# Two patterns of one pair of key heads, tile by tile in turn

## The chip, the cores and the metric

One core of a Trainium2 chip runs the whole program. The metric is the device time of one execution in microseconds, from the first to the last instruction with what the runtime puts around them. Inputs and outputs lie in HBM. The engines are TensorE (matmuls and transposes, into the eight banks of PSUM), VectorE, ScalarE and GpSimd for elementwise work, and SyncE, whose queue issues every DMA transfer of this kernel in program order: a transfer that has to wait for a semaphore holds up all that stand behind it.

## The reference, cut to what matters

Two sequences (256 and 512 tokens, 768 in all, six tiles of 128) go through two layers. Each layer normalises the tokens, projects them to the queries, keys, values and gates of three mixers, runs the mixers, gates their outputs, and adds the output projection. The change is about mixer C, whose heads use three patterns of keys and merge them by their softmax denominators:

```
C_PATTERNS = ((128, 1), (512, 4), (2048, 16))     # window, dilation
def dilated_mixture_attention(q, k, v, rel_bias):
    for g in range(N_C_GROUPS):
        idx = qpos[:, None] + offsets[g][None, :]
        valid = (idx >= 0) & (idx < S)
        s = jnp.einsum('bqhrd,bqkhd->bhrqk', qblk[:, :, g], kg) + biases[g]
        s = jnp.where(valid[None, None, None], s, NEG_INF)
        lse = jax.nn.logsumexp(s, axis=-1)
        p = jnp.exp(s - lse[..., None])
        outs.append(jnp.einsum('bhrqk,bqkhd->bqhrd', p, vg))
        lses.append(lse)
    alpha = jax.nn.softmax(jnp.stack(lses, axis=0), axis=0).transpose(0, 1, 4, 2, 3)
    return jnp.sum(jnp.stack(outs, axis=0) * alpha[..., None], axis=0)
```

Mixer C has 8 query heads and 2 key heads for each pattern (`KV_C` = 2), so each key head serves four query heads. Mixer A has a window of 128 tokens and 12 query heads, mixer B is dense with 12 query heads.

## The kernel before

A layer has three stages: the projection, the attention, and the output projection. The attention is a list of steps, worked through by all engines in a software pipeline. `attention_units` makes twelve units, each one key head of one pattern: first the four *quads* of mixer C's dilated patterns (unit 0 and 2 are dilation 4 for key head j = 0 and 1, unit 1 and 3 are dilation 16), then three units of mixer A, two of C's pattern of dilation 1, three of B. A quad unit has six items, one for each tile t of 128 queries, with all four heads at once; the other units have 12 items of two steps. That makes 24 quad steps (steps 0 to 23) and 192 others. The diff touches `attention_items`, which lays down the order of the items; nearly all else is worked out from it.

An item of dilation 4 is *open* (tokens of one residue mod 4 are in one tile, four heads of 128 by 128 scores, 512 columns). One of dilation 16 is *packed*: only keys of the same class count, so it has 128 columns for all heads.

TensorE at turn i of the loop does the score of step i (lines 1669, or 1674 and 1675), some pieces of the gate projection (lines 1644 to 1646, three matmuls each, `PIECES_BY` says how many are done by which turn: 14 between turns 0 and 23), the transposes of step i - 3 (line 1694), and the product with the values of step i - 4 (line 1734 open, 1715 packed). VectorE adds the bias and finds the minimum (`find_minima`: line 2225 four times for an open step; lines 2179 to 2186 for a packed one), ScalarE does the exponentials (lines 1901 and 1894). The transposed probabilities are copied out of PSUM (line 1154) by ScalarE for odd steps and by VectorE for even ones (`on_act`). The output of an open item is taken out by VectorE (`take_part`, line 2293), that of a packed one by ScalarE (`take_packed`, line 1928). Banks, `prob` and `part_out` are rings, of two banks for scores, two for transposes, two for products, four slots and eight slots. VectorE's work at turn i is `take_part` of step i - 5, `find_minima` of step i, the sums of a packed step i - 3, `pt_copy` of step i - 3.

SyncE's queue in the attention goes by items. For `it` from 4 on it does, in this order: `load_item(it)` (line 1309), which first waits until item `it - 4` is scored; `store_part` (line 1378) of the quad item nine places back; and what the tables `KEYS_AT` (`load_keys`, line 1237), `VALUES_IN_AT` (`load_values`, line 1254, or `load_blocks`, line 1273, for a packed unit), `BIASES_AT` (`load_bias`, line 1297) and `GATE_LOADS_AT` (gate weights, line 1189) give for that item. Keys and values have two slots (`KV_SLOTS`), bias sets two as well, so unit u takes the slot of unit u - 2:

```
KEYS_AT = at_items((u, UNIT_LAST[u - KV_SLOTS] + 1) for u in range(KV_SLOTS, len(ATT_UNITS)))
VALUES_IN_AT = at_items((u, UNIT_LAST[u - KV_SLOTS] + PAIR_LAG + 1) for u in range(KV_SLOTS, len(ATT_UNITS)))
BIASES_AT = at_items((b, BIAS_LAST[b - 2] + 1) for b in range(2, len(BIAS_SETS)))
```

`UNIT_LAST` is the last step of a unit, `UNIT_START` the first, `BIAS_LAST` the last step that uses a bias set, `PAIR_LAG` is 5. `at_items` turns a turn into the first item `it` whose item `it - 4` has its step at that turn or later. The scores of a unit's first step wait for its keys, `find_minima` for its bias, the first product (or the splits `values_hi` and `values_lo` in mixer A) for its values; `load_keys` itself waits until unit u - 2 has had its last score. Units 0 and 1 are loaded before the loop.

Of the kernel before, what the change touches and what calls it, by code (L numbers as in the profile page):

```python
# [44 lines left out]
KV_A, KV_B, KV_C = 3, 3, 2  # L45
# [238 lines left out]
def attention_units():  # L284
    def unit(kind, mixer, q, k, v, j, g, table, reach, bias_head, chunk):
        return dict(kind=kind, q=PLACE[q + 4 * j], k=PLACE[k + j], v=PLACE[v + j], j=j, g=g, table=table, reach=reach,
                    bias_head=bias_head, chunk=chunk + 2 * j)

    quads = [unit("Q", "C", U_QC + g * H_C, U_KC + g * KV_C, U_VC + g * KV_C, j, g, 2 * g, 0, H_A + g * H_C + 4 * j, 0)
             for j in range(KV_C) for g in (1, 2)]  # L290
    a = [unit("A", "A", U_QA, U_KA, U_VA, j, 0, 0, 1, 4 * j, 0) for j in range(KV_A)]
    c = [unit("C", "C", U_QC, U_KC, U_VC, j, 0, 1, 1, H_A + 4 * j, (H_A + H_B) // 2) for j in range(KV_C)]
    b = [unit("B", "B", U_QB, U_KB, U_VB, j, 0, None, 3, 0, H_A // 2) for j in range(KV_B)]
    return quads + a + c + b


ATT_UNITS = attention_units()
# [11 lines left out]
def packed(unit):  # L309

    return unit["kind"] == "Q" and unit["g"] == 2


def unit_items(u):
    return [(u, hp, t) for hp in ((None,) if ATT_UNITS[u]["kind"] == "Q" else (0, 1)) for t in range(TT)]


def attention_items():

    order = [x for u in range(len(ATT_UNITS)) for x in unit_items(u)]
    items, steps = [], []
    for u, hp, t in order:
        unit = ATT_UNITS[u]
        lo, hi = next(x for x in SEQ_TILES if x[0] <= t < x[1])
        a, b = max(lo, t - unit["reach"]), min(hi, t + unit["reach"] + 1)
        for r in (None,) if hp is None else (0, 1):
            first = min(max(t * P - C_REACH, lo * P), hi * P - C_KEYS) if unit["kind"] == "C" else a * P
            tiles = (1 if packed(unit) else 4) if r is None else C_KEYS // P if unit["kind"] == "C" else b - a  # L330
            steps.append(dict(item=len(items), u=u, unit=unit, kind=unit["kind"], hp=hp, t=t, r=r, a=a, first=first,
                              tiles=tiles, last=r != 0))
        items.append(dict(u=u, unit=unit, kind=unit["kind"], hp=hp, t=t, step=len(steps) - 1))
    return items, steps


ITEMS, STEPS = attention_items()

SHIFTED = sorted({x["first"] + j * P for x in STEPS if x["kind"] == "C" and x["first"] % P for j in range(x["tiles"])})
# [2326 lines left out]
```

How the kernel before makes its waits and increments, by code:

```python
        def prob_copied(eng, l, i):  # L914
            if features_first(STEPS[i]) or not on_act(i):
                eng.wait_ge(pt_dve, l * DVE_COPIES[-1] + DVE_COPIES[i])
            else:
                eng.wait_ge(pt_act, l * ACT_COPIES[-1] + ACT_COPIES[i])
# [1 line left out]
        def turn_evacuated(eng, i):  # L921
            l, s, t, b, _ = TURNS[i]
            if s == "norm":
                eng.wait_ge(norm_lo, NORM_AT[l, s, t, b] + 1)
            else:
                eng.wait_ge(turned_lo, HEAD_AT[l, s, t] + 1)
# [17 lines left out]
        def quad_taken(eng, l, quad):  # L945
            item = QUADS[quad]
            if packed(item["unit"]):
                eng.wait_ge(packed_taken, l * N_PACKED + item["packed_no"] + 1)
            else:
                eng.wait_ge(part_taken, l * (N_QUADS - N_PACKED) + item["open_no"] + 1)
# [5 lines left out]
        def bias_in(eng, l, b):  # L957
            sets = [x for x in BIAS_SETS if BIAS_NO[x] % 2 == b % 2]
            each_layer = sum(4 if x[1] is None else 2 for x in sets)
            in_layer = sum(4 if x[1] is None else 2 for x in sets if BIAS_NO[x] <= b)
            eng.wait_ge(bias_loaded[b % 2], 16 * (l * each_layer + in_layer))
# [5 lines left out]
        def stat_free(eng, pair):  # L968
# [3 lines left out]
            l, at = divmod(pair - STAT_SLOTS, N_PAIRS)  # L972
            old = PAIRS[at]
            if old["kind"] == "C":
                eng.wait_ge(merge_chain, 5 * (l * MERGES + old["merge_no"] // TT) + 5)
            else:
                eng.wait_ge(normed, l * NORMED[-1] + NORMED[old["step"]])
```

## Time and profile before

| | |
|---|---|
| median of three runs | 2769.77 us (2768.97 to 2772.97) |
| the profiled execution | 2773.48 us, span 2771.7 us |
| mean granted TensorE clock | 0.996 |
| quad steps, first quad score to first score of mixer A | 651.0 to 709.1 us, and 2028.4 to 2083.2 us |
| busy: TensorE, VectorE, ScalarE, GpSimd | 98%, 58%, 43%, 34% of the span |

A granted clock of 1.00 is the full 2.4 GHz, 0.50 is 1.2 GHz; a value between is a mean over a stretch. Engines' busy times overlap. "Releaser" is what ended an engine's idle time. A transfer's time to landing counts from the start of its issue to the semaphore that says it is there.

### The profile page before, as it was taken

What the parts mean: (1) busy time and instruction counts of PE and PEld (TensorE: products, weight loads), DVE (VectorE), ACT (ScalarE), POOL (GpSimd) and SP (SyncE); (2) the same over time, 40 slices, a digit from 0 to 9 for tenths busy, and PEclk for the clock granted to TensorE, in tenths of its full rate; (3) what the DMA queues carried; (4) which work ended last, traced back from release to release, by engine and by line L of the source; (5) the groups of instructions that cost most, each with busy time, mean ns of one, the idle gap of its engine ahead of it and who ended that gap; (6) DMA issues with size and microseconds to landing.
All of it is one profiled execution on the core that took longest, in us unless ns stands there. A gap on an engine that the chain in (4) does not pass through costs nothing. (4 is left out here: it accounts for less than half of the span.)

```text
span 2771.7 us, 43372 instructions
## 1 busy us (share of the span) xinstructions
PE 2728.9 (98%) x14505; PEld 2444.1 (88%) x14505; DVE 1614.7 (58%) x3901; ACT 1190.9 (43%) x2897; POOL 943.0 (34%) x864
## 2 busy tenths in 40 slices
PE   8999999999999999999999999999999999999999
PEld 7888899988999999988888888999889999998887
DVE  3345644434676677667743466444356766766776
ACT  4322222224565566544542222222256655664443
POOL 0333333320465377600003334333205743774000
PEclk9999999999999999999999999999999999999999
DMA  5366556658544443464524565666685345325535
GB/s 175 105 185 199 181 184 189 180 171 229 149 134 125 118 116 87 145 245 124 202 92 119 187 194 179 193 175 178 184 232 147 115 118 155 94 70 210 198 122 182
DMA packets 439415, 442.53 MB, mean 160 GB/s; under 512 B 103863, under 2 KB 333399, under 8 KB 439196
## 3 DMA queue, kind: packets, MB, share of 16 engines
q1 hardware_dynamic: 439196, 439.77, 53.0%
q8 instruction: 118, 1.93, 0.3%
q14 instruction: 101, 0.83, 0.1%
HBM read 313.91 MB, written 125.75 MB: 159 GB/s over the span
## 5 line engine op out<-in xcount | busy, mean ns | idle before, releaser
L1818 ACT CAST w_hi<-w_raw 128x512 fp32r<-128x512 f32 x640 | 397.2, 622 | 695.2 <-PE bank L1590 430.3
L1588 PE MATMUL bank<-w_hi,act_hi 128*128 128x512 f32 x1728 | 689.1, 399 | 0.0
L2099 DVE TENSOR_TENSOR w_lo<-w_raw,w_hi 128x512 fp32r<-128x512 f32 x640 | 457.8, 716 | 391.9 <-ACT w_hi L1818 389.0
L1590 PE MATMUL bank<-w_hi,act_lo 128*128 128x512 f32 x1728 | 679.0, 393 | 0.0
L1589 PE MATMUL bank<-w_lo,act_hi 128*128 128x512 f32 x1728 | 677.6, 392 | 0.0
L2548 POOL TENSOR_SCALAR prob<-prob,denom 128x256 f32<-128x256 f32 (+2 forms) x288 | 348.8, 1216 | 243.1 <-DVE denom L2263 239.8
L1590 PEld LDWEIGHTS bank<-w_hi,act_lo 128*128 128x128 f32 x1728 | 372.6, 216 | 54.0
L1588 PEld LDWEIGHTS bank<-w_hi,act_hi 128*128 128x128 f32 x1728 | 373.3, 216 | 50.0
L1589 PEld LDWEIGHTS bank<-w_lo,act_hi 128*128 128x128 f32 x1728 | 373.3, 216 | 48.8
L1644 PE MATMUL bank<-act_hi,w_hi 128*128 128x384 f32 x1024 | 348.8, 341 | 0.0
L1646 PE MATMUL bank<-act_hi,w_lo 128*128 128x384 f32 x1024 | 345.9, 338 | 0.0
L1645 PE MATMUL bank<-act_lo,w_hi 128*128 128x384 f32 x1024 | 345.6, 338 | 0.0
L1621 PE MATMUL bank<-w_hi,a_part 128*128 128x512 f32 x672 | 263.2, 392 | 5.7 <-DVE a_part L2391 3.0
L2254 DVE TENSOR_TENSOR pt_lo<-bank,pt_hi 128x256 fp32r<-128x256 f32 (+2 forms) x288 | 154.2, 535 | 188.3 <-ACT pt_hi L1920 186.2
L1622 PE MATMUL bank<-w_lo,a_part 128*128 128x512 f32 x672 | 261.7, 389 | 0.0
L1623 PE MATMUL bank<-w_hi,a_part 128*128 128x512 f32 x672 | 261.6, 389 | 0.0
L2539 POOL TENSOR_TENSOR y<-y,gains 128x256 f32<-128x256 f32 (+1 forms) x144 | 159.8, 1122 | 265.7 <-DVE y L2132 265.7
L2165 DVE TENSOR_TENSOR turned<-bank,turned 128x512 fp32r<-128x512 f32 (+2 forms) x120 | 64.8, 557 | 278.3 <-ACT turned L1885 278.2
L1885 ACT CAST turned<-bank 128x512 fp32r<-128x512 f32 (+2 forms) x120 | 55.3, 482 | 365.0 <-PE bank L1566 355.9
L1694 PE MATMUL bank<-ident,prob 128*128 128x128 f32 x1128 | 195.7, 274 | 5.7 <-POOL prob L2548 5.7
L1645 PEld LDWEIGHTS bank<-act_lo,w_hi 128*128 128x128 f32 x1024 | 193.9, 189 | 4.2
L1914 ACT ACTIVATE prob<-prob,minus_max 128x257 f32<-128x257 f32 (+2 forms) x240 | 128.2, 534 | 161.2 <-DVE minus_max L2245 160.4
(135 smaller groups left out, 4500.7 us busy)
## 6 DMA issues: line engine op xcount, KB each, us to landing
w_raw<-w_in SPq DMA_DIRECT2D x144, 512.0 KB, 4.8
w_sums<-sum_out SPq DMA_DIRECT2D x32, 1280.0 KB, 6.8
w_raw<-w_sums SPq DMA_DIRECT2D x80, 512.0 KB, 4.1
sum_in<-w_out SPq DMA_DIRECT2D x64, 512.0 KB, 5.6
heads_t<-turned SPq DMA_DIRECT2D x240, 128.0 KB, 2.4
q_t<-heads_t SPq DMA_DIRECT2D x192, 128.0 KB, 2.1
k_t<-keys_t SPq DMA_DIRECT2D x48, 384.0 KB, 5.8
w_raw<-w_out SPq DMA_DIRECT2D x32, 512.0 KB, 3.7
```

The lines of the kernel that those rows point to most:

```text
L1588: pe.matmul(acc[t][:], hi, w_hi[:, W_AT[n]:W_AT[n] + SLAB], start=(k == 0), stop=False)
L1589: pe.matmul(acc[t][:], hi, w_lo[:, W_AT[n]:W_AT[n] + SLAB], start=False, stop=False)
L1590: last = pe.matmul(acc[t][:], lo, w_hi[:, W_AT[n]:W_AT[n] + SLAB], start=False, stop=(k == KC - 1))
L1621: pe.matmul(bank[at][:], hi[:, tokens], w_hi[:, W_AT[n]:W_AT[n] + SLAB], start=(j == 0), stop=False)
L1622: pe.matmul(bank[at][:], hi[:, tokens], w_lo[:, W_AT[n]:W_AT[n] + SLAB], start=False, stop=False)
L1623: last = pe.matmul(bank[at][:], lo[:, tokens], w_hi[:, W_AT[n]:W_AT[n] + SLAB], start=False, stop=(j == KH - 1))
L1644: pe.matmul(out, hi, act_hi[:, k, tokens], start=(k == 0), stop=False)
L1645: pe.matmul(out, hi, act_lo[:, k, tokens], start=False, stop=False)
L1646: last = pe.matmul(out, lo, act_hi[:, k, tokens], start=False, stop=(k == KC - 1))
L1818: nc.scalar.copy(w_hi[:, W_AT[n]:W_AT[n] + SLAB], w_raw[:, load % W_RAW, j, :]).then_inc(w_hi_done, 1)
L2099: nc.vector.tensor_tensor(w_lo[:, W_AT[n]:W_AT[n] + SLAB], w_raw[:, load % W_RAW, j, :], w_hi[:, W_AT[n]:W_AT[n] + SLAB].bitcast(F32), ALU ...
L2548: nc.gpsimd.tensor_scalar(v, v, denom[:, pair % STAT_SLOTS, st["r"]:st["r"] + 1], None, ALU.mult)\
```

## The change

The items of unit 0 and unit 1 alternate tile by tile (open t = 0, packed t = 0, open t = 1, and so on), then those of unit 2 and 3; the rest of the list stays. Even quad steps are then open and odd ones packed. The items are the same and so is their work. All tables are worked out anew from the list: the first four values of `UNIT_START` and `UNIT_LAST` were 0, 6, 12, 18 and 5, 11, 17, 23, and are 0, 1, 12, 13 and 10, 11, 22, 23.

```diff
--- before.py
+++ after.py
@@ -319,7 +319,8 @@
 
 
 
-    order = [x for u in range(len(ATT_UNITS)) for x in unit_items(u)]
+    order = [x for j in range(KV_C) for both in zip(unit_items(2 * j), unit_items(2 * j + 1)) for x in both]
+    order += [x for u in range(2 * KV_C, len(ATT_UNITS)) for x in unit_items(u)]
     items, steps = [], []
     for u, hp, t in order:
         unit = ATT_UNITS[u]
```

## Rows read from the trace of the kernel before

**Rows 1.** The page: busy time of TensorE, share of the span, instructions.

```profile
PE 2728.9 (98%) x14505; PEld 2444.1 (88%) x14505; DVE 1614.7 (58%) x3901; ACT 1190.9 (43%) x2897; POOL 943.0 (34%) x864
```

**Rows 2.** Windows: us, then busy us (count) of each engine, granted clock, DMA share, GB/s.

```profile
651.00:709.10 58.10, 51.97 (x358) 48.30 (x356) 37.55 (x176) 30.03 (x128) 2.01 (x2) 0.89 0.83 233
709.10:715.00 5.90, 5.90 (x26) 5.50 (x25) 2.77 (x13) 2.23 (x7) 0.12 (x1) 0.65 0.31 82
2028.40:2083.20 54.80, 47.90 (x356) 44.63 (x355) 37.02 (x174) 29.38 (x127) 2.00 (x2) 0.96 0.86 246
2083.20:2088.00 4.80, 4.80 (x24) 4.62 (x23) 2.74 (x11) 2.51 (x9) 0.00 (x0) 0.78 0.36 94
```

**Rows 3.** Timeline of TensorE, layer 0: start us, duration us, line, operation.

```profile
663.82 0.61 PE L1669 MATMUL bank<-k_t,quad_t 128*128 128x64 f32 x4
664.27 0.42 PE L1644 MATMUL bank<-act_hi,w_hi 128*128 128x384 f32 x1
...
664.88 0.60 PE L1694 MATMUL bank<-ident,prob 128*128 128x128 f32 x4
665.32 1.00 PE L1734 MATMUL bank<-v_t,prob_t 128*128 128x64 f32 x8
666.13 0.39 PE L1669 MATMUL bank<-k_t,quad_t 128*128 128x64 f32 x2
```

**Rows 4.** Timeline of TensorE, layer 1: from one open score to the next.

```profile
2054.19 0.41 PE L1674 MATMUL bank<-k_t,quad_t 128*128 128x128 f32 x1
...
2055.60 0.41 PE L1674 MATMUL bank<-k_t,quad_t 128*128 128x128 f32 x1
```

**Rows 5.** Timeline of TensorE, layer 0: the first score of step 4.

```profile
658.68 0.33 PE L1674 MATMUL bank<-k_t,quad_t 128*128 128x128 f32 x1 [0.37 <-DMA quad_t<-heads_t]
```

**Rows 6.** Windows behind four waits, columns as in rows 2.

```profile
675.00:690.00 15.00, 14.27 (x72) 12.89 (x71) 8.76 (x55) 9.16 (x41) 0.00 (x0) 0.66 0.84 221
705.00:715.00 10.00, 8.61 (x34) 8.03 (x35) 4.66 (x19) 2.80 (x9) 0.12 (x1) 0.66 0.51 160
2062.00:2072.00 10.00, 8.77 (x61) 8.64 (x62) 7.06 (x35) 6.37 (x28) 0.00 (x0) 0.83 0.76 230
2077.00:2087.00 10.00, 7.41 (x38) 6.61 (x38) 4.87 (x18) 3.04 (x12) 0.00 (x0) 0.83 0.74 213
```

**Rows 7.** Timeline of SyncE's queue, layer 0: start us, us for the issues.

```profile
662.16 0.32 SPq L1309 DMA_DIRECT2D quad_t<-heads_t  x1
...
664.19 1.09 SPq L1237 DMA_DIRECT2D k_t<-keys_t  x2
...
692.66 3.71 SPq L1273 DMA_DIRECT2D blocks<-v_rows  x8
```

**Rows 8.** DMA issues, 655 to 716 us: count, KB each, median us to landing.

```profile
k_t<-keys_t SPq DMA_DIRECT2D x8, 384.0 KB, 5.8
...
v_t<-v_rows SPq DMA_DIRECT2D x2, 192.0 KB, 3.3
blocks<-v_rows SPq DMA_DIRECT2D x8, 24.0 KB, 2.5
bias<-bias_rows SPq DMA_DIRECT2D x4, 8.0 KB, 4.7
```

**Rows 9.** Landing of the `k_t` transfers, 655 to 716 us.

```profile
DMA to landing us min/median/max: 4.4/5.8/7.0
```

**Rows 10.** Timeline of VectorE, layer 0.

```profile
652.10 0.29 DVE L2225 CUSTOM_DVE_ANT_0 prob<-bank,bias 128x128 f32<-128x128 f32 x1 [3.68 <-PE bank L1675]
...
652.99 0.29 DVE L2225 CUSTOM_DVE_ANT_0 prob<-bank,bias 128x128 f32<-128x128 f32 x1
...
665.65 0.68 DVE L1154 COPY prob_t<-bank 128x512 f32<-128x512 f32 x1
666.36 0.42 DVE L2293 COPY part_out<-bank 128x256 f32<-128x256 f32 x1
666.78 0.29 DVE L2179 TENSOR_TENSOR prob<-bank,bias 128x128 f32<-128x128 f32 x1
```

## The prediction

> **What bounds the kernel now.** I read the page first: TensorE is busy for 98% of the span [rows 1]. Nothing else is near that, so a wait counts only where it stops TensorE, and then it counts in full. The edit touches the list of the first 24 items of each layer's attention, so I looked next at the two stretches in which TensorE works on them, from the first quad score to the first score of mixer A. They last 58.1 us in layer 0 and 54.8 us in layer 1 [rows 2]. The reader should see two things there: TensorE is idle for 6.1 and 6.9 us, which is rare in this kernel, and the granted clock is 0.89 and 0.96, and still 0.65 and 0.78 in the few microseconds behind. This is the only part with something to gain. TensorE's own work per step comes next: a packed score, a gate piece, the four transposes and the four products of an open item follow each other in 2.31 us (0.45, 0.61, 0.44, 0.81) [rows 3], and an open score with a packed item's transpose and product take 1.41 us [rows 4]. Last I read SyncE's queue and its transfers, since a step's queries, keys, bias and values all come through that one queue, in the order of the item list: `load_keys` for the second pair of key heads is issued in 1.09 us [rows 7] and lands 5.8 us after issue (4.4 to 7.0) [rows 8, 9].
>
> **What the change removes.** At best all that those stretches lose now. Layer 0: 58.10 - 51.97 = 6.1 us idle, 58.1 x 0.11 = 6.4 us through the clock, and 5.9 x 0.35 = 2.1 us just behind: 14.6 us. Layer 1: 6.9 + 54.8 x 0.04 + 4.8 x 0.22 = 10.2 us [rows 2]. Together 24.8 us. A regular mix of long and short steps may well cure it: the present waits are for a queue that falls behind short steps and for an engine that falls behind long ones. I credit the whole, and put what may remain under a term of its own.
>
> **What it adds: late loads.** No instruction is added. But `UNIT_LAST` of the first four units changes from 5, 11, 17, 23 to 10, 11, 22, 23, while `UNIT_START` changes from 0, 6, 12, 18 to 0, 1, 12, 13. Only two units' keys fit at a time, and the queue asks for the next only when the unit before last has had its last step. Worked through `at_items`: keys and bias of unit 2 stood at item 10 of the queue and now stand at item 15; unit 3 stays at 16; unit 4 goes from 22 to 27. Values: unit 2 from 15 to 20, unit 3 stays at 21, unit 4 from 27 to 30. Item n's own load waits for the score of item n - 4, so keys of unit 2 are now requested after score 11 and needed by score 12; keys of unit 3 after score 12, needed by score 13 (it was 18); keys of unit 4 after score 23, needed by 24; values of unit 2 after score 16, needed by product 12, which is TensorE's next task but a transpose; values of unit 3 after score 17, needed by product 13. Six loads that had about five steps of cover have less than one. Each price below is for one layer: issue, landing, less the work TensorE still has.
>
> Ahead of them in the queue are one query load (0.32 us) and one part store (taken alike, some 0.4 us with its pause): 0.9 us from the score to the first key transfer, 0.55 us to the second [rows 7], 5.8 us to land, 0.1 us to start.
> Keys of unit 2: 0.9 + 0.55 + 5.8 + 0.1 = 7.3 us, less a gate piece, four transposes and a packed product (0.61 + 0.44 + about 0.25, and a little pipelining): **5.9** (4.5 to 7.1).
> Keys of unit 3: the same 7.3 us, less one transpose and an open product (0.9 us): **6.4** (5.0 to 7.6).
> Bias of unit 3 goes out behind those keys and lands 4.7 us later [rows 8]; VectorE waits at `find_minima` 13, and behind that wait stand `pt_copy` 10 and with it TensorE's product 10: **1.1** (0 to 2).
> Values of unit 2: 0.9 + 3.3 [rows 8] + 0.1 less 0.2: **4.1** (3.4 with the 2.5 us of the small blocks, 5.3 with the keys' shortest landing).
> Blocks of unit 3: 0.9, then eight issues in 3.71 us, the last 3.2 us after the first [rows 7], 2.5 us to land [rows 8], 0.1, less a gate piece and four transposes (0.9): **5.9** (5.4 to 6.7).
> Keys of unit 4: as unit 2: **5.9** (4.5 to 7.1).
> Values of unit 4: after score 29 0.9 + 3.3 + 0.1, then the splits on ScalarE and VectorE, about 1.1 us for both (the wider copy takes 0.68 [rows 10]), against 3.3 us of gate pieces, transposes and score 30: **2.1** (1.2 to 3.2).
> First queries: item 4's load lets TensorE start at 658.68 [rows 5] whatever stands before it, and the shorter steps 1 and 3 leave it less to do until then: **1.6** (0 to 2.5).
> The sum is 33.0 us a layer (24.0 to 41.5).
>
> **The clock.** After today's waits the granted clock sits between its two levels of 2.4 and 1.2 GHz on average: 0.66 over 15 us, 0.66 over 10, 0.83 over 10 and 0.83 over 10 [rows 6], which costs 5.1, 3.4, 1.7 and 1.7 us, on average 3.0. The new waits are longer than those. Three of them (unit 3's keys, unit 3's blocks, unit 4's keys) are followed by plain work and I charge 3.0 each; the other two long ones run into the next wait, which hides half of it: 1 each. That is 11 us a layer (5.1 to 17.3).
>
> **VectorE.** Open items now have even numbers, so all their 512-wide copies fall to VectorE (0.68 us [rows 10]), none to ScalarE. A pair of steps costs it 0.89 + 4 x 0.29 with pauses (1.25) + 0.68 + 0.42 [rows 10] and 0.28 for the packed sums: 3.5 us, against 1.41 + 2.31 = 3.7 us of TensorE. That just fits, at no cost, while the two stay in step; for a missed beat, a weight split (three in this stretch) or a part store that is late for its slot I charge 3 us a layer (0 to 8).
>
> **Sum.** 33.0 + 11 + 3 = 47.0 us a layer, 94.0 in all, less 24.8: +69 us. The profiled execution took 2773.5 us around a span of 2771.7, 3.7 above the median of 2769.8; the difference is set on the median: **2839 us**. All low ends give 2 x 29.1 - 24.8 = +33, or 2803; all high ends 2 x 66.8 - 24.8 = +109, or 2879.
>
> A page speaks on this too. The Trainium skill, "DMA: Bandwidth & Descriptors", Anatomy of one DMA, has about 2.0 us fixed plus the bytes at 436 GB/s (for the GpSimd path). By it both key transfers together would be down in an estimated 3.8 us where rows 8 and 9 show 5.8 after a second issue 0.55 us late, and the values in 2.4 instead of 3.3: 9 us a layer less, and a result of about 2820. The rows were taken beside this kernel's other traffic, so I stay with them.
>
> **Rivals.** (1) *Only the score waits show.* The value loads arrive in time because the queue has caught up by then and TensorE is held elsewhere. Per layer 1.6 + 5.9 + 6.4 + 1.1 + 5.9 = 20.9, clock 7, beats 3: 30.9; twice, less 24.8: +37, 2807 us. For it: their landings are short. Against it: the request hangs on scores 16 and 17, not on the queue's leisure. (2) *VectorE sets the pace.* If a pair takes 4.5 us instead of 3.7, 12 pairs cost 9.4 us a layer, of which 3 are charged: +13 in all, 2852 us. For it: 3.5 against 3.7 leaves nothing. (3) *Faster.* The even mix gives back 24.8 us, and the loads hide as they do now: 2 x (1.6 + 3) - 24.8 = -16, 2754 us. It would need keys that land within the 1.3 us that TensorE still has, or a request that goes out earlier than I read. It decides from the point where waits and clock cost under 12.4 us a layer; the two key waits at steps 12 and 13 alone come to 9.5 at their shortest. (4) *They cancel* near that point, within 5.5 us.
>
> **Chances.** Forecast 0.74, rival 1 0.13, rival 2 0.08, rival 3 0.03, rival 4 0.02. A measurement here tells about 0.2% (5.5 us) from no change. Faster 0.03, same 0.02, slower 0.95. The range runs from the low ends and rival 1 to some way above rival 2: 2803 to 2865.
>
> **What would show it.** In the chain of waits: TensorE idle until a transfer of `k_t` some 5 to 7 us before score 12, again before 13, again before 24 (the first of mixer A), in both layers; idle for `v_t` before product 12, for `blocks` before product 13. The stretches should be about 85 us long, with the granted clock low behind each wait, and between the waits a pair of steps should take about 3.7 us with TensorE back to back; the waits for `quad_t` in the middle of packed runs should be gone. From mixer C on nothing should differ. I am wrong if keys of unit 2 are in SyncE's timeline before score 11 is done; if the waits are there but short, the landing is mis-sized; if steps 4 to 11 already run late, VectorE is.

## The result

The changed kernel takes 2844.74 us (median of 4 runs, 2839.69 to 2847.02) where the kernel before takes 2771.37 beside it (2768.97 to 2780.37): ratio 1.0254, interval 1.0235 to 1.0273, some +70 us. The forecast was +69 and 2839, with 0.95 on slower. The profiled execution took 2839.69 us around a span of 2837.9, 66.2 us more than the span before. It is the fastest of the four; where the other three lose 5 to 7 us more, at a mean granted clock of 0.980 or 0.981 against 0.982, no trace shows.

The page of the changed kernel comes first. TensorE's busy time rose by only 16.3 us against [rows 1], with the same number of instructions. Most of the loss is therefore idle time, and the rest is the same work at a lower clock.

```profile
PE 2745.2 (97%) x14505; PEld 2458.7 (87%) x14505; DVE 1616.5 (57%) x3901; ACT 1189.5 (42%) x2897; POOL 943.3 (33%) x864
```

The windows from the first quad score to the first score of mixer A, and the 20 us behind, in both layers (columns as in [rows 2]; the stretches end at the same score as there, but two of the four products that still lie behind that score are now open ones):

```profile
650.60:735.10 84.50, 56.50 (x342) 52.33 (x340) 39.39 (x179) 30.58 (x132) 2.02 (x2) 0.72 0.60 162
735.10:755.00 19.90, 17.00 (x99) 16.33 (x100) 7.81 (x34) 6.70 (x22) 6.64 (x7) 0.89 0.61 161
2058.90:2144.10 85.20, 55.72 (x342) 51.65 (x340) 39.24 (x179) 30.59 (x132) 2.02 (x2) 0.75 0.59 160
2144.10:2164.00 19.90, 17.20 (x98) 16.55 (x99) 7.74 (x33) 6.70 (x22) 6.64 (x7) 0.88 0.62 162
```

The stretches grew by 26.4 and 30.4 us. That is 56.8 of the 66.2; the other 9.4 lie close behind, in mixer A. In layer 0 a load of gate weights issued at 765.54 before stands at 796.13 now, 30.6 us later, and the keys issued at 1034.09 stand at 1064.70, still 30.6 us later: between the two nothing more is lost. In the two stretches TensorE is idle for 28.0 and 29.5 us, where it was idle for 6.1 and 6.9, and the granted clock is 0.72 and 0.75 instead of 0.89 and 0.96.

These are the waits of TensorE in the changed kernel: what it waited for, the total in us, how often, the longest.

```profile
PE bank L1675 <- issue: 13.6, 2, 6.9
PE bank L1670 <- issue: 12.3, 2, 6.2
PE bank L1681 <- issue: 10.9, 2, 5.5
PE bank L1735 <- DMA v_t<-v_rows: 10.3, 2, 5.9
PE bank L1716 <- DMA blocks<-v_rows: 8.5, 2, 4.3
...
PE bank L1750 <- issue: 6.0, 4, 2.9
```

None of the first five is in the kernel before; each comes twice, once in each layer. (Lines are one higher than before.) L1675 is the open score, here that of step 12; L1670 the packed score, here step 13; L1681 the first score of mixer A, step 24; L1735 and L1716 are the products of steps 12 and 13. Where the row says only "issue", the profile names no releaser. SyncE's timeline does: keys are requested at 671.50, just as TensorE runs out of work, and again at 681.84, after score 12.

```profile
670.66 0.32 SPq L1310 DMA_DIRECT2D quad_t<-heads_t  x1
671.03 0.43 SPq L1379 DMA_DIRECT2D part_rows<-part_out  x1
671.50 1.09 SPq L1238 DMA_DIRECT2D k_t<-keys_t  x2
...
681.84 1.10 SPq L1238 DMA_DIRECT2D k_t<-keys_t  x2
```

TensorE's side of it (timeline, start and duration in us, the idle time before in brackets):

```profile
671.52 0.60 PE L1716 MATMUL bank<-blocks,prob_t 128*128 128x256 f32 x2
679.01 0.45 PE L1675 MATMUL bank<-k_t,quad_t 128*128 128x128 f32 x1 [6.89 <-issue]
...
688.86 1.03 PE L1670 MATMUL bank<-k_t,quad_t 128*128 128x64 f32 x4 [6.08 <-issue]
...
705.97 0.87 PE L1735 MATMUL bank<-v_t,prob_t 128*128 128x64 f32 x3 [4.36 <-DMA v_t<-v_rows]
...
714.94 1.19 PE L1716 MATMUL bank<-blocks,prob_t 128*128 128x256 f32 x2 [4.26 <-DMA blocks<-v_rows]
...
735.01 0.55 PE L1681 MATMUL bank<-k_t,q_t 128*128 128x256 f32 x1 [5.40 <-issue]
```

From the first key issue at 671.50 to the score at 679.01 are 7.5 us: a second issue 0.55 us later, and a landing near the top of its spread (4.2 to 6.9 us for `k_t` in this stretch). What the transfers took, 655 to 735 us (KB each, median us from issue to landing), answers to [rows 8]:

```profile
k_t<-keys_t SPq DMA_DIRECT2D x6, 384.0 KB, 5.6
...
v_t<-v_rows SPq DMA_DIRECT2D x1, 192.0 KB, 3.5
blocks<-v_rows SPq DMA_DIRECT2D x8, 24.0 KB, 1.9
```

The granted clock in four windows of layer 0: before the first new wait, from the end of that wait on, behind that, and at the start of mixer A.

```profile
660.00:671.40 11.40, 11.25 (x90) 11.01 (x91) 9.23 (x45) 7.22 (x32) 0.00 (x0) 1.00 0.70 203
679.00:719.00 40.00, 25.30 (x104) 23.58 (x105) 12.03 (x55) 8.31 (x34) 0.00 (x0) 0.50 0.42 107
719.00:730.00 11.00, 10.43 (x81) 9.63 (x80) 9.10 (x37) 7.75 (x34) 0.00 (x0) 1.00 0.54 167
735.00:739.40 4.40, 4.39 (x18) 4.30 (x19) 0.91 (x5) 1.27 (x4) 0.00 (x0) 0.51 0.02 5
```

Before the wait the alternating steps run at 2.4 GHz; behind it TensorE works at 1.2 GHz for 40 us, through the next three waits and all the work between. Then it is back at 2.4 GHz until the wait for unit 4's keys, and low once more for 4.4 us behind that. At half rate 25.3 us of work should have taken 12.65, and 4.39 should have taken 2.2: 14.8 us for layer 0. In layer 1 three stretches at 0.50, 0.52 and 0.54 (2087.5 to 2101, 2112 to 2133, 2144 to 2149.5) hold 7.25, 16.75 and 5.50 us of work, by the same reckoning 14.2 us.

Now the books close: the waits of both layers come to 61.1 us (worked out below), the clock to 29.0, and the 24.8 us that the kernel before lost here are gone or included: 65.3, against 66.2 between the spans.

### The profile page after: what moved, and what is told of

The parts are those of the page before. It is cut to its first block and busy times, and to the rows that moved or that the text cites. A ratio compares the mean times of both kernels' runs of the same rounds, so it can differ in the third digit from the quotient of the medians.

```text
span 2837.9 us, 43376 instructions
## 1 busy us (share of the span) xinstructions
PE 2745.2 (97%) x14505; PEld 2458.7 (87%) x14505; DVE 1616.5 (57%) x3901; ACT 1189.5 (42%) x2897; POOL 943.3 (33%) x864
## 5 line engine op out<-in xcount | busy, mean ns | idle before, releaser
L1645 PEld LDWEIGHTS bank<-act_hi,w_hi 128*128 128x128 f32 x1024 | 194.3, 190 | 4.1
```

Source lines behind the costliest of these rows:

```text
L1645: pe.matmul(out, hi, act_hi[:, k, tokens], start=(k == 0), stop=False)
```

## The experiments

Ratios are to the kernel before on the same chip, each kernel timed in five rounds. What an expectation calls the changed kernel is the one above.

### One pair at a time

**e1_first_pair** alternates units 0 and 1 only.

```diff
-    order = [... for j in range(KV_C) for both in zip(...) ...]
+    order = [x for both in zip(unit_items(0), unit_items(1)) for x in both]
+    order += [x for u in (2, 3) for x in unit_items(u)]
...
```

> Only units 0 and 1 alternate; units 2 and 3 stay one after the other. Late-load theory: unit 2's keys (asked for after score 11, needed by score 12) and unit 2's values are late as in the changed kernel, unit 3's and unit 4's loads are early again. TensorE idle some 6.8 us before score 12 and 4 to 6 us before product 12 in each layer, none before score 13, product 13 or score 24: +28 us against the kernel before (18 to 38). Pace theory (alternation itself is slow, for VectorE or for the copies that all fall to one engine): half of the whole loss, about +36 us, spread over steps 0 to 11 and none of it at step 12.

Measured: 2797.73 us, ratio 1.0092 (1.0066 to 1.0117), about +25. Its waits:

```profile
PE bank L1676 <- issue: 14.3, 2, 7.7
PE bank L1736 <- DMA v_t<-v_rows: 11.4, 2, 5.7
```

**e2_second_pair** is the mirror: units 0 and 1 in sequence, 2 and 3 alternating.

> Only units 2 and 3 alternate. Late-load theory: unit 2's loads are early, unit 3's keys (before score 13) and blocks (before product 13) and unit 4's keys (before score 24) and values are late: some 18.7 us idle and 9 us of low clock a layer, less the 8 us that this half lost before: +39 us (28 to 50), and with the first pair's alone it adds up to the whole loss of 73 us within 10. Pace theory: +36 us, the same as the first pair's alone.

Measured: 2819.12 us, 1.0165 (1.0139 to 1.0191), about +46. Its waits:

```profile
PE bank L1671 <- issue: 14.4, 2, 7.6
PE bank L1717 <- DMA blocks<-v_rows: 12.1, 2, 6.4
...
PE bank L1682 <- issue: 8.5, 2, 4.4
```

Each half brings exactly the waits of the loads whose slots its pair holds on to: the first pair unit 2's keys and values; the second unit 3's keys and blocks and unit 4's keys and values (the last as two waits of up to 2.6 us at L1751). 0.92% and 1.65% make 2.57%, the whole change 2.54%: the halves add up.

### How much head start a load needs

**e3_one_ahead**, **e4_three_ahead** and **e8_four_ahead** let the open unit run one, three or four tiles ahead of the packed one. Its slot then comes free that many steps earlier.

```diff
-    order = [... for j in range(KV_C) for both in zip(...) ...]
+    order, ahead = [], 3          # 1 in the first, 4 in the last
+    for j in range(KV_C):
+        wide, narrow = unit_items(2 * j), unit_items(2 * j + 1)
+        order += wide[:ahead] + [x for both in zip(wide[ahead:], narrow) for x in both] + narrow[TT - ahead:]
...
```

> Alternating, but the open item runs one tile ahead of the packed one, so each late load is asked for one score earlier (two scores before its use instead of one). Late-load theory: each wait is shorter by one step, 1.5 to 2.3 us, so 17 us idle a layer instead of 30, and less low clock: +32 us (15 to 50). Pace theory: five sixths of the alternation is left, so about +60 us.

Measured: 2813.74 us, 1.0138 (1.0114 to 1.0162), about +38. The waits for keys of units 2 and 3 fell to 4.51 and 5.18, 4.42 and 3.94 us, that for values to 2.82 and 3.13, the blocks' to 0.6, and that for unit 4's keys to 1.69 and 3.67.

> The open item runs three tiles ahead, so each load is asked for four scores before its use, some 8 us, against 7.3 us from request to landing. Late-load theory: no wait on k_t, v_t or blocks above 1 us; the time falls to that of the kernel before or under it, -10 us (-25 to +6). Pace theory: half of the alternation is left, about +36 us.

Measured: 2772.83 us, 0.9986 (0.9972 to 1.0000). That is 4 us of gain where I had expected 10. Three waits for keys are above the 1 us that I had allowed: one of 1.20 us before the first score of unit 2 in layer 1 (the profile names no releaser, but SyncE had issued these keys 8 us before), and two for unit 4's keys, shown below. Small ones for queries (1.37 and 0.40 us) and blocks (0.56 us) remain beside them.

```profile
PE bank L1684 <- DMA k_t<-keys_t: 2.3, 1, 2.3
PE bank L1684 <- issue: 2.3, 1, 2.3
```

> Four tiles ahead: five scores between request and use, one third of the alternation left. Late-load theory: no wait on keys or values above 0.5 us; -6 us against the kernel before (-20 to +5). If the alternation itself helps by its even mix, this has less of it than three tiles ahead, and comes out no faster than that.

Measured: 2775.27 us, 1.0007 (0.9995 to 1.0019). One tile ahead gives back 32 us, three the whole loss, and a fourth nothing more: all new key waits are gone, but small waits for queries, for VectorE's copies and a low clock (0.78 over layer 1's stretch of 63.1 us) take their place. I had asked for more than the order can give.

### The same order without the late loads

**e5_alt_loads_out** lets units 2 and 3 compute on the keys, bias and values of units 0 and 1, so those loads are left out; all steps and their work stay. **e6_seq_loads_out** does the same in the order before. Both leave the right keys, bias and values of units 2 and 3 out, so only their times are of use.

```diff
-                        load_keys(l, u)
+                        if u > 3:
+                            load_keys(l, u)
...
-                        load_values(l, u)
+                        if u > 3:
+                            load_values(l, u)
...
-                        load_bias(l, b)
+                        if b > 3:
+                            load_bias(l, b)
```

> The changed kernel, but units 2 and 3 use the keys, bias and values of units 0 and 1: their loads are left out, and with them the four waits inside the quad steps; unit 4's keys and values stay late. Late-load theory: of 30 us idle a layer about 8 are left (before score 24 and in mixer A), with some 3 us of low clock and 3 to 5 of small waits, against 12.4 that the kernel before loses: +8 us in all (-10 to +20). Pace theory: the loss is in the steps themselves, so +50 us or more stays.

Measured: 2772.05 us, 0.9993 (0.9983 to 1.0003). Its windows:

```profile
650.20:701.90 51.70, 44.36 (x342) 41.57 (x341) 38.61 (x179) 30.27 (x132) 2.00 (x2) 1.00 0.74 215
2025.60:2077.30 51.70, 44.45 (x342) 41.65 (x341) 38.76 (x179) 30.19 (x132) 2.02 (x2) 0.96 0.74 216
```

and the only key wait left, before score 24, for the load that stayed:

```profile
PE bank L1684 <- issue: 11.4, 2, 5.8
```

> The kernel before with the same loads left out (units 2 and 3 use the keys, bias and values of units 0 and 1). It tells what leaving them out is worth by itself. Late-load theory: in the old order they were hidden, only the traffic beside the query loads gets less: -6 us (-15 to +3). If the transfers themselves fill the DMA engines and set the pace, more than -20 us.

Measured: 2763.47 us, 0.9963 (0.9948 to 0.9978).

The same 24 alternating steps take 51.7 us instead of 84.5, at a clock of 1.00 in layer 0; 5.7 us of that are the wait for unit 4's keys, so the steps themselves need 46.0. The order costs nothing as an order, and the 73 us of the whole hang on the loads of units 2 and 3. Two things keep this pair from being the whole proof. Leaving these loads out also takes their traffic away, which e6 prices at 10 us in the order before. And with them out the alternating order is 8.6 us slower than the old one (2772.05 against 2763.47): its waits for unit 4's keys, 11.4 us, and values, up to 3.3 us each, are still there. That it is the lateness and not the traffic is shown by e4 above and e9 below, in which every load is made and the loss is gone too.

### Keys ahead of the queries in the queue

**e7_three_ahead_keys_first** is e4 with an item's `load_keys` put before its query load and part store.

> Three tiles ahead, and in SyncE's queue the keys of the next unit are asked for before the item's own queries and the part store, 0.8 us sooner. Late-load theory: the wait of 2.3 us before score 24 shrinks to about 1.5 in each layer, some low clock behind it goes: 2 to 5 us under three tiles ahead alone. Pace theory: no difference.

Measured: 2771.80 us, 0.9992 (0.9981 to 1.0003), so no gain over e4: a miss. The key wait before score 24 did go, but one of 1.41 us for that item's own queries (`q_t`) stands there instead, layer 1's stretch was granted 0.86, and products wait for VectorE's copies (4.3 us over the kernel at L1738, 3.0 in e4).

### The slots filled by halves

**e9_alt_half_loads** keeps the alternating order and loads keys and values of units 2 to 4 in two halves of three tiles, each asked for as soon as its own three tiles have been used. The two small packed bias tables get a tile of their own, so that bias no longer needs a slot of the pair. **e10_seq_half_loads** is its control: the same loads in the order before.

```diff
+def freed(u, g, lag):
+    if u > 4:
+        return UNIT_LAST[u - KV_SLOTS] + lag
+    return min(i for i, st in enumerate(STEPS) if st["u"] == u - KV_SLOTS and st["t"] == 3 * g + 2) + min(lag, V_LAG + 1)
...
-KEYS_AT = at_items((u, UNIT_LAST[u - KV_SLOTS] + 1) for u in range(KV_SLOTS, len(ATT_UNITS)))
+KEYS_AT = at_items(((u, g), freed(u, g, 1)) for u in range(KV_SLOTS, len(ATT_UNITS)) for g in range(2))
...
-BIASES_AT = at_items((b, BIAS_LAST[b - 2] + 1) for b in range(2, len(BIAS_SETS)))
+BIAS_SLOT = [0, None, 1, None] + [b % 2 for b in range(4, len(BIAS_SETS))]
```

> Alternating as in the changed kernel, same work and same two slots, but keys and values are loaded in two halves of three tiles, each as soon as the steps of those tiles are done, and the packed units' small bias tables lie apart, so that unit 2's bias can be loaded at the start. Each half is asked for five scores or more before its use. Late-load theory: no wait of TensorE on k_t, v_t or blocks above 0.5 us, quad stretches of some 47 us at full clock instead of 84: 2751 us, -20 against the kernel before (-28 to -8). Pace theory: +50 us or more stays. DMA theory (the transfers fill the engines): stretches stay at 55 us, time as before.

Measured: 2766.38 us, 0.9979 (0.9965 to 0.9993). All waits for `k_t`, `v_t` and `blocks` are gone with the alternating order intact, which is what the theory needed; but the gain was 6 us where I had forecast 20. What took the rest is in its waits and in SyncE's timeline:

```profile
PE bank L1700 <- DMA quad_t<-heads_t: 5.8, 3, 2.8
```

```profile
674.15 1.18 SPq L1253 DMA_DIRECT2D k_t<-keys_t  x2
675.37 2.13 SPq L1313 DMA_DIRECT2D bias<-bias_rows  x2
677.55 0.43 SPq L1327 DMA_DIRECT2D quad_t<-heads_t  x1
```

The queries of step 14 stand behind 3.3 us of issues of one item. TensorE waits 2.73 and 2.80 us for them, and is granted 0.71 over the 17 us from 683 on. In layer 1 of this profiled execution TensorE also waits 1.70 us for VectorE, until 2026.89, and is granted 0.55 over the next 5 us and 0.64 over 8 more. VectorE had itself been idle for 5.28 us until a transfer landed. It is no wait for queries, and e11's profiled execution does not have it.

> The same half loads and bias places in the order of the kernel before. Late-load theory: its loads were hidden already, so this is the control: 0 us (-8 to +5). If the half loads and not the order made the alternating one fast, both gain alike.

Measured: 2778.41 us, 1.0001 (0.9980 to 1.0023), with a wide spread from 2762 to 2788. In its profiled execution, the slowest of the twelve, layer 1 paid dearly for one wait of 2.25 us for `quad_t` at 2037.56. The 20 us behind it, with TensorE never idle:

```profile
2040.00:2060.00 20.00, 20.00 (x86) 19.25 (x84) 9.72 (x31) 3.87 (x11) 0.00 (x0) 0.50 0.62 174
```

Five gate pieces lie in these 20 us; this is the first matmul of the first:

```profile
2042.81 0.67 PE L1667 MATMUL bank<-act_hi,w_hi 128*128 128x384 f32 x1
```

**e11_alt_half_loads_spread** is e9 with the wide bias of number 4 asked for at another item of the queue, so that it no longer piles up in front of step 14's queries.

```diff
-BIASES_AT = at_items((b, BIAS_LAST[BIAS_OLD[b]] + 1) for b in range(4, len(BIAS_SETS)))
+BIASES_AT = at_items((b, 18 if b == 4 else BIAS_LAST[BIAS_OLD[b]] + 1) for b in range(4, len(BIAS_SETS)))
```

> The alternating kernel with half loads, with one load moved: the bias of mixer A's first half, which held SyncE's queue for 2.1 us right behind unit 2's second half of keys, goes out seven items later. In the kernel with half loads TensorE's one long wait in each layer, 2.7 to 2.8 us for item 14's queries, stands there, with low clock for 10 us behind it. Queue theory: that wait falls under 1 us and the low clock goes, 8 us less in each layer, 2752 us, -20 against the kernel before (-26 to -8). If instead the DMA engines are simply full at that place, the wait stays and the time is that of the kernel with half loads, -6.

Measured: 2760.49 us (2758.90 to 2762.00), 0.9953 (0.9940 to 0.9966): 13 us faster than the kernel before, some 84 than the changed one; I had forecast 20. Its windows and what is left of the query waits (1.5 us at the longest, where I had expected under 1):

```profile
650.20:701.80 51.60, 49.02 (x342) 46.15 (x340) 38.36 (x179) 30.08 (x131) 2.02 (x2) 0.90 0.83 243
2021.70:2071.00 49.30, 45.73 (x340) 42.88 (x339) 37.77 (x178) 29.80 (x130) 2.01 (x2) 0.97 0.86 255
```

```profile
PE bank L1700 <- DMA quad_t<-heads_t: 1.8, 2, 1.5
```

Once its loads have cover, the alternating order thus gains about half of the 24.8 us of losses. Half loads alone, in the order before, were worth nothing (e10); whether they would be with the bias moved as well was not tried, so how much of e11's 13 us is the order's alone stays open.

### Other work put into the waits

**e12_gate_work_in_the_waits** leaves the order and loads of the changed kernel alone, and moves the 14 gate pieces, which are spread over the quad steps, to steps 11 and 12, where TensorE waits.

```diff
-    cost = [3 if packed(st["unit"]) else {"Q": 1}.get(st["kind"], 8) for st in STEPS]
+    cost = [(24 if i in (11, 12) else 0) if st["kind"] == "Q" else 8 for i, st in enumerate(STEPS)]
```

> The changed kernel with its late loads, but the 14 gate pieces of the quad steps all stand behind scores 11 and 12, seven each, where TensorE waits for the keys of units 2 and 3. Late-load theory: 12 of the 14 pieces, 6.2 us, now run inside the two waits instead of beside other steps, the waits shrink from 6.8 and 6.1 to some 3.3 and 2.6 us, and the clock does not fall before the values' wait, 2 to 5 us more: -8 to -11 us a layer, 2825 us against 2844 (2818 to 2833). If the time from request to landing were not what TensorE waits for, moving its work would change nothing, or lengthen the other steps' latencies and cost time.

Measured: 2852.41 us, 1.0284 (1.0267 to 1.0300), 8 us above the changed kernel where I had forecast some 20 below: a miss. The waits before scores 12 and 13 did shrink, from 25.9 us in all to 10.3:

```profile
PE bank L1675 <- issue: 6.6, 2, 4.5
```

But the steps that had lost their gate pieces ran at half the clock. Windows of layer 0: until the clock had fallen, while it was low, its last half microsecond, and behind its rise, which comes before the first gate piece:

```profile
651.10:657.00 5.90, 5.01 (x35) 4.49 (x35) 4.66 (x26) 3.26 (x16) 0.00 (x0) 0.85 0.62 178
657.00:674.50 17.50, 17.50 (x80) 16.96 (x80) 10.28 (x46) 8.64 (x37) 2.00 (x2) 0.50 0.62 183
675.00:675.50 0.50, 0.50 (x5) 0.50 (x5) 0.00 (x0) 0.00 (x0) 0.00 (x0) 0.50 0.02 4
676.00:676.90 0.90, 0.90 (x11) 0.90 (x10) 0.90 (x10) 0.40 (x2) 0.00 (x0) 1.00 0.25 23
```

```profile
676.97 0.42 PE L1645 MATMUL bank<-act_hi,w_hi 128*128 128x384 f32 x1
```

TensorE had no idle time in those 17.5 us; the longest wait in the 6 us before was one of 0.70 us for VectorE, which ended at 653.22. In the changed kernel the same steps, with their gate pieces, kept 1.00. Layer 1 is alike: 0.50 from 2070 to 2090, and the first gate pieces, from 2091.90 on, run at 1.2 GHz too. Over the two stretches TensorE is busy for 67.4 and 66.8 us with the work that took 56.5 and 55.7 in the changed kernel: 22 us more, against 12 us less in the waits for late loads (61.6 us in all there, 49.6 here).

## Why the prediction was right

Forecast +69 us, measured about +70 by the ratio and +73 by the medians. The mechanism was the forecast one: without the loads of units 2 and 3 the alternating order costs nothing (e5), and neither with them when they are asked for earlier (e4, e9).

**Late loads.** Six waits stand where the six were forecast. Forecast, then layer 0 and layer 1, in us: keys of unit 2 5.9, measured 6.89 and 6.67; keys of unit 3 6.4, measured 6.08 and 6.20; values of unit 2 4.1, measured 4.36 and 5.92; blocks of unit 3 5.9, measured 4.26 and 4.25; keys of unit 4 5.9, measured 5.40 and 5.46; values of unit 4 2.1, measured 2.90 and about 2.7. Together 30.3 forecast, 29.9 and 31.2 measured. The values of unit 2 in layer 1 lie above their range of 3.4 to 5.3: they landed in 5.0 us, where I had taken 3.3. The queue had issued a 512 KB load of gate weights (L1190) just ahead of them, 2 us before; in layer 0, where `v_t` landed in 3.5 us, that load was 4.5 us ahead. That it slowed them is likely, but was not tried.

```profile
2104.80 0.43 SPq L1190 DMA_DIRECT2D w_raw<-w_in  x1
...
2106.87 0.38 SPq L1255 DMA_DIRECT2D v_t<-v_rows  x1
```

The blocks lie below their range of 5.4 to 6.7, for two reasons that the rows show: they land in 1.9 us instead of 2.5, and TensorE had 2.0 us of work left (708.7 to 710.68) instead of 0.9, since by then it worked at the low clock. The half clock hides a part of the very transfers that brought it about.

**The two small terms.** First queries 1.6 and bias of unit 3 1.1: measured 0.3 and nothing. Both were too high, by 2.4 us a layer. Product 10 stands in the timeline without a wait, right behind the transpose.

**The clock.** Forecast 11 us a layer (5.1 to 17.3), measured 14.8 and 14.2. The term was inside its range but under-sized, and the step that failed is the reasoning behind it: I priced one recovery per wait from [rows 6], at a mean of 3.0 us. In layer 0 the clock did not recover between the first four waits: one low stretch of 40 us ran through the work between them, and only before unit 4's keys was it up again. In layer 1 it recovered once more, between the waits for unit 3's keys and unit 2's values (0.97 from 2101 to 2106).

**VectorE.** Forecast 3 us a layer for missed beats, measured none to speak of. In the 11.4 us before the first new wait TensorE is busy for 11.25 (the window above). One pair of steps there, from an open score to the next:

```profile
663.78 0.41 PE L1675 MATMUL bank<-k_t,quad_t 128*128 128x128 f32 x1
...
664.80 0.39 PE L1645 MATMUL bank<-act_hi,w_hi 128*128 128x384 f32 x1
...
666.75 0.42 PE L1645 MATMUL bank<-act_hi,w_hi 128*128 128x384 f32 x1
...
668.05 0.41 PE L1675 MATMUL bank<-k_t,quad_t 128*128 128x128 f32 x1
```

That pair takes 4.27 us because it holds two gate pieces; the one before it, with one, takes 3.63, against 3.7 forecast. VectorE's 3.5 us fit beneath. Rival 2 is out, and e5 says the same for the whole section.

**What it removes.** All 24.8 us were credited. The waits for `quad_t` in front of packed scores, 7.7 us in all in the chain of waits of before, are down to 0.2, as forecast. This is their row in the kernel before:

```profile
PE bank L1669 <- DMA quad_t<-heads_t: 7.7, 4, 3.3
```

Of the idle time the credit was near the truth: outside the forecast waits TensorE is idle for 1.0 us in each stretch, where it was idle for 6.1 and 6.9. The other 11.8 us of the 24.8 were low clock, and the trace cannot tell old low clock from new. e11 gets 13 us in all, after its own remaining waits and a clock of 0.90 and 0.97.

**The sum.** The errors cancelled: the clock 3.5 us a layer too low, first queries, bias and beats together some 5 too high. That the total came within 2 us of the ratio's +70 is in that part luck; that the six waits came out right is not. Rival 1, only the score waits, fell with the rows of `v_t` and `blocks`: 10.3 and 8.5 us. Rival 3 needed a request that goes out earlier; e4, e9 and e11 are that rival made true, and e11 reached -13 of its -16 us. e4 and e8, at 0.9986 and 1.0007, are where rival 4 stood: losses and gains cancel.

**The page's figure.** The Trainium skill, "DMA: Bandwidth & Descriptors", Anatomy of one DMA, gave an estimated 3.8 us for the two key transfers of a unit (its fit is for the GpSimd path) and with it some 2820 us in all. The rows after show a median of 5.6 us for `k_t` and 3.5 for `v_t` from SyncE's queue beside this kernel's traffic. The measured landings decide, and the sum by them was nearer by some 20 us.

## What to carry to other kernels

Two units that alternate hold both of two slots until the pair's end, so that nothing can be prefetched for the next pair: when two streams are interleaved, count for each load the steps between the release of its slot and its first use, before counting what the mix gains. The cure is to release and fill slots by parts (here halves, with the bias loads moved, which turned +73 us into -13) or to let one stream lead; and then see what else the queue issues at the same place, since 3.3 us of issues in front of one query load cost e9 about half its gain. Filler work moved into a wait is missed where it came from: in e12 the steps without it ran at half the clock, and the kernel lost more than the shorter waits gave.

## What the runs showed of the hardware

- After one wait, work in which TensorE was never idle stayed at the lower level of 1.2 GHz for long: 17.5 us of quad steps without gate pieces in e12, 20 us in e10. It can be short as well: behind the 5.40 us wait before mixer A's first score the changed kernel was back at 2.4 GHz from 739.4 on, 4.4 us after that score began. That the gate pieces are what keeps it up is only a reading of e12 against the changed kernel, and two rows speak against the simple form of it: e10's 20 us at 1.2 GHz hold five gate pieces, and in layer 0 of e12 the clock was up by 676.0, before the first gate piece at 676.97. What decides it stays open.
- The waits ahead of a fall need not be long. The clock fell after 0.70 us (e12), 2.25 us (e10) and 2.7 us (e9).
- The order in which a queue issues can matter with the same transfers: e9 and e11 differ only in the item at which one bias is asked for, and that was worth 7 us by their ratios (0.9979 and 0.9953).
